# Spread loads, turn-taking between first weight casts and first-tile roots on GpSimd, and a reordered last part of stage 6

## Time and profile before

| | |
|---|---|
| median of 3 runs | 2918.89 us (2918.82 to 3147.31) |
| the profiled execution's own time | 2915.52 us |
| its span on the slowest core (core 5) | 2914.0 us; the eight cores 2908.6 to 2914.0 us |
| granted TensorE clock, mean by core | 0.994 or 0.995 |
| busy: TensorE / VectorE / ScalarE / GpSimd | 97% / 68% / 47% / 24% |
| chain that ended last | TensorE 89%, VectorE 4%, issue 3%, DMA 2% |

### The profile page before, as it was taken

One profiled execution on the slowest core, in us unless ns is written; L12 is line 12 of the kernel. 1 busy time (PEld: TensorE's weight loads), 2 busy tenths in 40 slices (PEclk: granted clock), 3 DMA queues, 4 the chain that ended last, 5 costly groups with the idle time before them and its releaser, 6 DMA issues.

```text
span 2914.0 us, 53868 instructions; the slowest of 8 cores (2908.6 to 2914.0 us)
## 1 busy us (share of the span) xinstructions
PE 2833.8 (97%) x15980; PEld 1454.5 (50%) x15980; DVE 1994.9 (68%) x3101; ACT 1360.3 (47%) x2595; POOL 712.9 (24%) x1137
## 2 busy tenths in 40 slices
PE   6999998999999999999999999999999999999998
PEld 3555543444455555444446555444445655544443
DVE  4767663566767777766677778776667787766566
ACT  5767641232456664233256665323235666532222
POOL 3333222131122222222222222113113231211211
PEclk9999999999999999999999999999999999999999
DMA  7786547973653324475483222448356323244344
GB/s 188 129 141 120 109 88 187 245 209 116 180 137 79 82 66 106 132 227 149 130 216 86 73 75 72 127 146 256 109 158 180 82 68 75 72 145 143 130 121 150
DMA packets 349980, 386.54 MB, mean 133 GB/s; under 512 B 209136, under 2 KB 222960, under 8 KB 349184
## 3 DMA queue, kind: packets, MB, share of 16 engines
q1 hardware_dynamic: 336160, 357.72, 43.6%
q0 software_dynamic: 13536, 25.37, 6.3%
HBM read 298.70 MB, written 65.60 MB: 125 GB/s over the span
## 4 chain that ended last, share of the span: by engine, by line
PE 89%; DVE 4%; issue 3%; DMA 2%; ACT 1%; SPq 1%; DVEq 0%; POOL 0%; ACTq 0%; POOLq 0%
PE ps L479 89%; DVE sb_CS L505 1%; DVE sb_CS L509 1%; DMA sb_GR<-x 1%; SPq L536 1%; DMA sb_onT<-sb_ON 0%; DMA sb_W<-wsc 0%; ACT sb_AT L496 0%; DVE sb_GR L505 0%; ACT sb_CS L496 0%; DMA wsc<-sb_W 0%; DVE sb_onT L509 0%; DVE sb_G L505 0%; DVE sb_TF L509 0%; DVE sb_TB L509 0%
## 5 line engine op out<-in xcount | busy, mean ns | idle before, releaser
L479 PE MATMUL ps<-sb_uT,sb_W 128*128 128x512 bf16 (+2 forms) x7840 | 1633.0, 366 | 7.2 <-DMA sb_W<-wsc 5.4
L479 PEld LDWEIGHTS ps<-sb_uT,sb_W 128*128 128x128 bf16 (+1 forms) x7840 | 708.2, 98 | 814.9 <-issue 32.0
L496 ACT ACTIVATE sb_CS<-ps 128x512 f32<-128x512 f32 (+2 forms) x512 | 272.9, 538 | 656.5 <-PE ps L479 443.8
L505 DVE TENSOR_TENSOR sb_CS<-ps,sb_CS 128x512 f32<-128x512 f32 (+1 forms) x464 | 314.6, 688 | 241.4 <-PE ps L479 166.7
L479 PE MATMUL ps<-sb_GR 128*128 128x512 bf16 (+2 forms) x1792 | 348.0, 318 | 0.7 <-DVE sb_AT L523 0.6
L509 DVE SCALAR_TENSOR_TENSOR sb_CS<-sb_CS,sb_convw 128x512 f32<-128x512 bf16 x256 | 209.9, 824 | 94.3 <-ACT sb_CS L496 82.6
L514 POOL TENSOR_SCALAR sb_stat<-sb_stat 128x1 f32<-128x1 f32 (+1 forms) x257 | 76.5, 298 | 758.8 <-ACT sb_TB L496 371.7
L479 PE MATMUL ps<-sb_onT,sb_W 128*128 128x512 bf16 x1024 | 243.0, 381 | 12.1 <-DVE sb_onT L509 12.1
L479 PE MATMUL ps<-sb_V,sb_uT 128*128 128x256 bf16 x2048 | 238.1, 274 | 0.0
L479 PEld LDWEIGHTS ps<-sb_GR 128*128 128x128 bf16 x1792 | 163.8, 98 | 137.5 <-issue 1.7
L479 PEld LDWEIGHTS ps<-sb_V,sb_uT 128*128 128x128 bf16 x2048 | 200.4, 98 | 30.6 <-issue 0.7
(11 more groups left out here) (138 smaller groups left out, 3202.7 us busy)
## 6 DMA issues: line engine op xcount, KB each, us to landing
sb_W<-wsc SPq DMA_DIRECT2D x412, 256.0 KB, 2.7
sb_W<-wst SPq DMA_DIRECT2D x168, 256.0 KB, 2.9
sb_onT<-x SPq DMA_DIRECT2D x56, 512.0 KB, 5.7
sb_GR<-x SPq DMA_DIRECT2D x44, 512.0 KB, 6.0
sb_W<-w_all POOLq DMA_DIRECT2D x80, 256.0 KB, 6.4
wsc<-sb_W SPq DMA_DIRECT2D x80, 256.0 KB, 5.8
y<-sb_GR SPq DMA_DIRECT2D x36, 512.0 KB, 4.0
sb_ycT<-x SPq DMA_DIRECT2D x28, 512.0 KB, 5.4
```

Of the source, the lines that this page charges most:

```text
L479: S.add("pe", lambda e: e.matmul(out, lhsT=lhsT, rhs=rhs, start=start, stop=stop, skip_group_check=more), r, w, cost=max(0.025, free_n(rhs ...
L496: S.add("act", lambda e: e.activation(out=out, in_=in_, func=func, **kw), r, w, table=TABLE.get(func), cost=0.17 + 0.82e-3 * free_n(in_) + ...
L505: S.add(eng, lambda e: e.tensor_tensor(out=out, in0=a, in1=b, op=op), r, w, cost=ecost(eng, free_n(out), narrow(out, a, b)))
```

## The change

It leaves the arithmetic as it is, except for the order of some operations. By parts:

1. Start: x tile 0 is loaded first, then ident, gpre and tiles 1 to 7, with meta and gbias behind tile 5. Tiles 8 to 15 each wait for the square of the tile five places before (a wait on the chip). The first casts are tied to the roots in turn: k behind the root of tile 0, q behind tile 1, lr behind 2, v behind 3, cc, cx, z, cb behind 5 to 8, and the next root waits (in the planned order, hence in GpSimd's queue) for the cast before it. The gate weights `wg` are loaded behind v, and the bias is negated behind tile 6.
2. `sums_w` uses three pairs of buffers in `AT` in turn instead of one pair in `CS`; the first two gates of the plain stage wait for the last use of `AT` by head 3.
3. `finy`: the multiplication that ended p3 is done behind p7's addition.
4. `merge` moves d = 6 to GpSimd; conditions of the merges name the products accordingly.
5. `load_wo` becomes four loads of 512 KB behind the mb unit of d = 2, 3, 4, 5 in stage 6 of half 0, and behind the last transpose of head 3.
6. Tiles 1 to 3 of the next sequence are loaded behind the cb unit of conv 2, 3, 4 of half 1; tile 0 as before.

```diff
-        const(gbias[:], gbias_d, "gbias")
         load_x0(0)
+        const(ident[:], ident_d, "ident")
         const(gpre[:], gpre_d, "gpre")
-        const(ident[:], ident_d, "ident")
...
+EARLY = {("k", 0): 0, ("q", 0): 1, ("lr", 0): 2, ("v", 0): 3, ("cc", 0): 5, ("cx", 0): 6, ("z", 0): 7, ("cb", 0): 8}
...
-                put("W" + self.name, lambda: self.load(n), None,
-                    [("SA", 0, {"W1": 1, "V": 2, "W2": 3}[self.name])] if n == 0 else after)
+                put("W" + self.name, lambda: self.load(n), ("WL", blk) if first and blk in EARLY else None, [("SB", 0, EARLY[blk])] if first and blk in EARLY else after)
...
-            dma("sp", xv, x_d[0, i * 128:(i + 1) * 128, :], [], xk, ("xs", i), 1 << 19)
+            dma("sp", xv, x_d[0, i * 128:(i + 1) * 128, :], [], xk, ("xs", i), 1 << 19, [G["sq", i - 5]] if i >= 8 else ())
...
-        dma("pool", wg[:], wg_d, [], ["wg"], "cw", 1 << 18)
+        put("X0", lambda: dma("pool", wg[:], wg_d, [], ["wg"], "cw", 1 << 18), None, [("WL", ("v", 0))])
+        put("X0", lambda: ts("dve", ngb[:], gbias[:], -1.0, None, ALU.mult, ALU.bypass, ["gbias"], ["ngb"]), "wg", [("SC", 0, 6)])
...
-            S1, S2 = sd1(BF16, 0, 512), sd1(BF16, 512, 512)
-            S4, S3 = sd2(BF16, 0, 512), sd2(BF16, 512, 512)
+            turn = G.get("wst", 0) % 3
+            G["wst"] = G.get("wst", 0) + 1
+            tmp = [Buf("AT", turn * 4096 + z * 2048, 2048) for z in range(2)]
+            S1, S2 = tmp[0](BF16, 0, 512), tmp[0](BF16, 512, 512)
+            S4, S3 = tmp[1](BF16, 0, 512), tmp[1](BF16, 512, 512)
...
                 tt("dve", s_ap, bk[0][:, 0:512], s_ap, ALU.add, bk[1] + s_k, s_k)
+                if (f, s) == (0, 1):
+                    G["late", d] = (s_ap, s_k)
+                    return
+                if (f, s) == (1, 1):
+                    l_ap, l_k = G.pop(("late", d))
+                    b_ap, b_k = ta[1](F32)
+                    stt(b_ap, b_ap, 1.0, l_ap, ALU.add, ALU.mult, l_k + b_k, b_k)
                 stt(a_ap, a_ap, 1.0, s_ap, ALU.add, ALU.mult, s_k + a_k, a_k)
...
-                tt("dve" if d > 5 else "pool", m_ap, t_ap, a_ap, ALU.add, t_k + a_k, m_k)
+                tt("dve" if d > 6 else "pool", m_ap, t_ap, a_ap, ALU.add, t_k + a_k, m_k)
...
-                    a.append(("og", b - 1, 0, 7, 1))
+                    a.append(("cb", (b - 1, 1, 1 + i), 1) if 1 <= i < 4 else ("og", b - 1, 0, 7, 1))
...
-                put("SB", lambda i=i: sbf(i), ("SB", b, i), [("SA", b, i)])
+                put("SB", lambda i=i: sbf(i), ("SB", b, i),
+                    [("SA", b, i)] + ([("WL", w) for w, n in EARLY.items() if n == i - 1] if b == 0 else []))
...
-            put("LW", lambda b=b: load_wo(b), None, [("O", b, 3, 0, 7)])
+            for p in range(4):
+                put("LW", lambda b=b, p=p: load_wo(b, p), ("wo", b, p), [("O", b, 3, 0, 7), ("X", b, 3, 7), ("mb", b, 0, p + 2, 1)])
```

More of the change, by code:

```diff
@@ L417, in program @@
         for c in ("M", "BO", "BS", "BX", "RM", "BM", "BN", "EM", "ES2", "ES3", "ES", "EN", "C", "SC", "SB", "SA", "ST", "F2", "F1", "WW1", "WV", "WW2",
-                  "LW", "L", "MG", "TY", "TT", "D1", "D2"):
+                  "LW", "X0", "L", "MG", "TY", "TT", "D1", "D2"):
             LS.chain(c)
@@ L533, in mset, with dma @@
             S.add(eng, lambda e: e.memset(ap, val), [], w)
-        def dma(q, out, in_, r, w, semkey, nbytes):
-            return S.add(q, lambda e: e.dma_start(out=out, in_=in_), r, w, semkey=semkey, nbytes=nbytes)
+        def dma(q, out, in_, r, w, semkey, nbytes, extra=()):
+            return S.add(q, lambda e: e.dma_start(out=out, in_=in_), r, w, extra=extra, semkey=semkey, nbytes=nbytes)
         def dtr(out, in_, r, w, semkey, nbytes):
@@ L709, in program @@
             load_x0(i)
-            if i == 3:
+            if i == 5:
                 dma("sp", xm_ap, meta_d, [], xm_k, ("xm",), 65536)
-        dma("pool", wg[:], wg_d, [], ["wg"], "cw", 1 << 18)
+                const(gbias[:], gbias_d, "gbias")
+        put("X0", lambda: dma("pool", wg[:], wg_d, [], ["wg"], "cw", 1 << 18), None, [("WL", ("v", 0))])
+        put("X0", lambda: ts("dve", ngb[:], gbias[:], -1.0, None, ALU.mult, ALU.bypass, ["gbias"], ["ngb"]), "wg", [("SC", 0, 6)])
         for (dst, src, key) in [(smask[:], smask_d, "smask"), (convw[:], convw_d, "convw"), (maskb[:], maskb_d, "maskb"),
@@ L715, in program @@
             const(dst, src, key)
-        ts("dve", ngb[:], gbias[:], -1.0, None, ALU.mult, ALU.bypass, ["gbias"], ["ngb"])
         uTm = Buf("MT", 0, 256)
@@ L1220, in phase1 @@
                         if meta:
-                            put("F1", lambda s=s: meta_gate(s), ("mg", s), [("lr", 0, 0)] + ([("ms", s - 1)] if s else []))
+                            put("F1", lambda s=s: meta_gate(s), ("mg", s), ["wg", ("lr", 0, 0)] + ([("ms", s - 1)] if s else []))
                             put("M", meta_kin, None, [("mg", s), ("k", 0, s, 0, 1)])
@@ L1224, in phase1 @@
                             put("M", lambda s=s: meta_state(s), ("ms", s), [("v", 0, s, 0, 3)] + ([("P", 0, s - 1, 1, 3)] if s else []))
-                        aft = [("lr", b, half)]
+                        aft = [("lr", b, half)] + ([] if b else ["wg"])
                         if b and s == 0 and half == 0:
@@ L1385, in sums_w @@
             tt("dve", S3[0], x1, y1, ALU.subtract, xk1 + yk1, S3[1])
-            for z, bf in enumerate((sd1, sd2)):
+            for z, bf in enumerate(tmp):
                 ap, k = bf(BF16)
-                dma("sp", ssrc(pair, z), ap, k, [("wst", pair, z)], ("ws", pair < 8, z), 1 << 18)
+                dma("sp", ssrc(pair, z), ap, k, [("wst", pair, z)], ("ws", turn, z), 1 << 18)
         class Seven:
@@ L1539, in stage6 @@
                             units[n, s] = (lambda n=n, s=s, d=d, hm=hm: gate(hm[n], d, s, n, hm["ma"]), (n, b, hh, d, s),
-                                           [("mt", b, hh, d - 2, z) for z in range(2)] if d > 1 else [])
+                                           [("mt", b, hh, d - 2, z) for z in range(2)] if d > 1 else [("qm", 0, 3, 1, 1)])
                         for n in ("oc", "og"):
@@ L1583, in stage6 @@
                         put("MG", lambda d=d, z=z, s=s: merge(d + z, s), ("mt", b, hh, d + z, s),
-                            [("og", b, hh, d + z, 1 - s), ("oc", b, hh, d + z, s if z == 0 else 1 - s)])
+                            [("og", b, hh, d + z, 1 - s), ("oc", b, hh) + {(0, 0): (d, 0), (0, 1): (d + 1, 0), (1, 1): (d + 1, 0), (1, 0): (d + 1, 1)}[z, s]])
         def cast_wo(d):
@@ L1590, in cast_wo, with load_wo @@
             dma("pool", src(wsc_d), src(w_d), [], [("wsc", "wo", d)], ("woc", d), 3 << 18)
-        def load_wo(b):
-            ap, k = woB(BF16)
-            dma("sp", ap, wsrc(wsc_d, ("wo", 0)), [("wsc", "wo", d) for d in range(8)], k, ("wo",), 1 << 21)
+        def load_wo(b, p):
+            ap, k = woB(BF16, p * 2048, 2048)
+            dma("sp", ap, wsrc(wsc_d, ("wo", 0))[:, p * 2048:(p + 1) * 2048], [("wsc", "wo", d) for d in (2 * p, 2 * p + 1)], k,
+                ("wo", p), 1 << 19)
         def stage7(b, hh):
@@ L1647, in stage7 @@
                 me = (b, hh, il)
-                tiles.append((lambda il=il: tile(il), ("t7",) + me, [("mt", b, hh, d, at(il) // 4) for d in range(8)]))
+                tiles.append((lambda il=il: tile(il), ("t7",) + me, [("mt", b, hh, d, at(il) // 4) for d in range(8)] + [("wo", b, p) for p in range(4)]))
                 put("EN", lambda il=il: norm(il), ("n7",) + me, [("t7",) + me])
@@ L1678, in sa @@
                 G["s0", i] = sq_stat(*buf(i), *us(i))
+                G["sq", i] = S.ops["act"][-1]
             def sbf(i):
```

## The result

The changed kernel takes **2888.4 us** against 2918.9 us (medians of 4 runs each); the ratio is 0.990, 95% interval 0.988 to 0.992. That is faster by 1.0%, inside the 2% band; the forecast was 2891 in a range of 2868 to 2919. The interval is 0.4% wide, so the measurement tells far smaller differences than the 2% that the prediction names. The profiled execution took 2888.13 us with a span of 2886.6 (core 4), 27.4 less than before (core 5). What remains to be seen is whether the five terms of the sum are the ones that made it.

What follows compares the result with a forecast made beforehand. TensorE was taken as the bound, busy 2833.8 of 2914.0 us, leaving at most 80 us idle to gain. Terms -11 + 2 - 6 - 7 - 6 = -28 us against the 2918.9 median gave 2891 us, range 2868 to 2919.

Steps and rivals of the forecast that it cites:

- wo load, -11 + 2: Wait for onT near 446 us shrinks, -11 us; the load moved into the plain stage costs +2 us.
- no stall is left: Best end of the wo load's range: the onT stall goes wholly, -14 us.
- rival (c): Plain stage becomes bound by DMA, late weight blocks cost 7.5 us each, 2949 us with 8 late; chance 7%.
- Next tiles, -6: Near 571 us, weights come 5.2 us earlier without three of four x tiles ahead: -6 us, ends -7.5 and 0.
- End of stage 6, -7: Last pair of seven stages 6: the 1.08 us wait before p4 goes, -7 us, ends -7.6 and +2.
- p4 starts without a wait: One pair earlier in stage 6, with merges on GpSimd, p4 has no wait; the last pair gets that state.
- The upper end: End of stage 6, +2 us: slower d = 6 merges on GpSimd (1.26 for 0.69 us) delay stage 7's first tile.
- Start, -6: First 60 us: tile 3 at 16 to 17 us instead of 20.20, -6 us, ends -14.6 and +8.
- may double or go: Idle time of 60 to 430 us, 7 us, may double or go as the planner orders everything anew.
- Rival (d): Start gives the whole 14.6 us and small waits of 60 to 430 us fall away: 2875 us; chance 9%.
- Rival (a): Start gains nothing or loses, casts coming late and DMA engines full anyway: 2897 to 2905 us; chance 16%.
- (b): Stalls at 446 and 571 us come from stores and casts, not bursts, and stay: 2908 us; chance 10%.

Runs made afterwards that it cites:

- experiment 3: Kernel before with only the wo load changed to four loads behind the last transpose: 2912.8 us, ratio 0.9983.
- experiment 9: Changed kernel with wo again one 2 MB load, ready when the first half of head 3 is done: median 2885.6 us, ratio 0.9904.
- experiment 2: Kernel before with only the start changed (part 1): median about 2907 us, ratio 0.9987, of the medians 0.996.
- experiment 1: Changed kernel with the start (part 1) put back as before: median 2894 us, ratio 0.9951, of the medians 0.992.
- Experiment 10: Changed kernel with the planner's assumed landing time of a transposing DMA raised from 3.5 to 5.0 us, only the written order moving: 2902 and 2904 us.
- experiment 6: Kernel before with only tiles 1 to 3 of the next sequence loaded one by one behind conv units: 2912 us, ratio 0.9981.
- experiment 8: Changed kernel with the first casts not tied to the roots, load order and held tiles 8 to 15 kept: 2893.6 us, ratio 0.9919.

## Why the prediction was right, and which terms were not

The total is right (2888.4 for 2891, -27.4 in the span for -28), and the stalls that the parts were to remove are gone. But of the five sizes three are off, and they cancel; that the sum came out within 1 us in the span is in part luck.

- **wo load, -11 + 2.** In the trace -14.1 + 1.8, the end "no stall is left". But the cause in the whole is not part 5: alone it gives 5 us (experiment 3), and without it nothing is lost (experiment 9). The planner's new order, which part 1 brings, takes the stall away by itself (experiment 2). The prediction treated the parts as independent; two of them removed the same stall. The price in the plain stage was sized right; rival (c), a plain stage bound by DMA, showed as one late cast: the share rose from 0.80 to 0.92, without more.
- **Next tiles, -6.** -7.5 by the stretch, -5 to -6 alone: right.
- **End of stage 6, -7.** Parts 3 and 4 alone gave 10 us; the changed kernel gains 1.77 us a stage in the six later ones, 12.4 for seven, of which about 3 us are the order's. The mis-sized step is "p4 starts without a wait" for the pairs with merges on GpSimd: they hid 0.2 us each, which part 3 took away. The upper end came too, small: stage 7's first tile waits for `GR` from VectorE in three of the stages, 1.5 us in all, and before in none. A GpSimd merge still holds VectorE up (0.69 us without one), as these rows of the changed kernel show:

```profile
2824.35 1.26 POOL L505 TENSOR_TENSOR sb_GR<-sb_G 128x512 bf16<-128x512 f32 x1
2824.75 1.42 DVE L509 SCALAR_TENSOR_TENSOR sb_G<-sb_G,sb_CS 128x512 f32<-128x512 f32 x1
```

  It costs nothing that shows on the path: the moved merges alone gained 5 us. These two rows agree with the rule of the Trainium skill, SBUF — State Buffer, section "SBUF: two separate sides", by which one of two such operations waits for the other; the kernel's time does not go by it here.
- **Start, -6.** Taking part 1 out costs 6 us (experiment 1), but not for the reason given. The first 60 us give 12.2 (tile 3 at 13.64 instead of the 16 to 17 forecast), near the end of -14.6, and phase 1 takes about 17.5 back: by the stretches the start has lost some 5 us. The step that failed is the sentence that idle time of 60 to 430 "may double or go", which stands in no term of the sum: it grew from 7 to 18 us, and the clock took 7 us more. Experiment 10 shows that it is the order that does this. What part 1 is worth lies behind phase 1. Experiment 1 loses 29.2 + 3.6 at the start (idle time and clock), 8.4 + 3.7 in phase 1, 4.3 + 3.5 at `onT` and 2.1 + 1.8 for a cast, 56.6 together; the changed kernel 20.3, 17.75 + 9.0, 0.2 and 1.8, together 49.1. Up to 425 us that is 44.9 for 47.1, and the gain is the stall and the cast. The balance gives 7.5 us where the spans differ by 6.6.
- **Sum.** -12.2 + 17.5 - 14.1 + 1.8 - 7.5 - 12.4 = -26.9, against -27.4 measured. Rival (d) had the start right and phase 1 wrong. Rival (a) is out as to its reason, since the start came 12.2 us earlier, though its result, no gain from the start by itself, is what phase 1 made of it; (b) is out by experiments 3 and 6. Of the signs named as right all came but the 95 us without a gap; of those named as wrong two came, new waits in 60 to 430 and a wait for a cast in the plain stage.

Open: why the planner's model puts the attention steps too close in the new order, that is, which of its assumed times is too short, was not tried.

## What to carry to other kernels

Where a planner writes the order, a part's price has two terms: what it does in its own place, and what the new order does everywhere else; the second was here the larger one (+17 in phase 1, and -14 at `onT`, for -12 in the start's own place), and only single-part runs tell them apart. A gain that two parts share must be counted once: put each part in alone and take each out alone. And compare the starts of TensorE's instructions, not the idle times alone, where gaps of 0.2 us repeat: here they were worth some 4 us in seven stages (2908 for 2912.4).

## What the runs showed of the hardware

- With four casts issued by GpSimd at 2.36 us (and the gate weights at 1.58), beside the x tiles on SP's queue, the square of the second tile stood at 13.36 us instead of 10.74 and that of the fourth at 19.36 instead of 13.64 (experiment 8 against the changed kernel). Casts spread between the roots left the weights in time: TensorE's one wait for a cast there is 1.8 us in the plain stage.
- Waits of TensorE of 1.85 to 4.34 us in phase 1 stood in stretches of 20 us at a granted clock of 0.91, which is 3.6 of the 20 us at the lower level of 0.50; one of 1.80 us (near 319) and, in the kernel before, one of 2.59 us stood at 1.00, as did all the waits of 1.08 us.
